# Latent attention by pairs of heads: another order of work on TensorE, VectorE and ScalarE

## What is computed

```python
def mla_queries(h, w_q_a, q_a_norm, w_q_b, q_nope_norm, q_rope_norm, cos, sin):
    c_q = rms_norm(h @ w_q_a, q_a_norm)
    q = (c_q @ w_q_b).reshape(bsz, seq, N_HEADS, QK_DIM)
    q_nope = rms_norm(q[..., :QK_NOPE_DIM], q_nope_norm)
    q_rope = apply_rope(rms_norm(q[..., QK_NOPE_DIM:], q_rope_norm), ...)
...
    def one_block(args):
        s = jnp.einsum('bhqd,bhkd->bhqk', q_blk, k).astype(jnp.float32) * scale
        s = jnp.where(key_pos[None, :] <= query_pos[:, None], s, NEG_INF)
        p = jax.nn.softmax(s, axis=-1).astype(v.dtype)
        return jnp.einsum('bhqk,bhkd->bhqd', p, v)
...
            o = causal_block_attention(q, k_shared, v_shared)
            x = x + o @ mla_w_o[j]
```

## Time and profile before

| | |
|---|---|
| median of 3 runs | 1831.97 us (1831.77 to 1832.18) |
| the profiled execution | 1831.05 us, of which 1829.2 us are its span |
| TensorE busy | 1752.6 us, 96% of the span |
| VectorE, ScalarE busy | 68%, 51% |
| the stretch from the first unit to the third column of the output product | 599.98 to 811.14 us |

### The profile page before, as it was taken

The page is one execution under the profiler, slowest core; times in us unless marked ns, Lnnn a source line. Parts: engine busy times, 40 slices in busy tenths (PEclk is TensorE's granted clock), DMA queues, the critical chain, the costliest instruction groups (busy, mean ns, idle before and its releaser), DMA issues.

```text
span 1829.2 us, 27614 instructions
## 1 busy us (share of the span) xinstructions
PE 1752.6 (96%) x10382; PEld 1430.3 (78%) x10382; DVE 1239.3 (68%) x1895; ACT 926.6 (51%) x1692; POOL 486.0 (27%) x383
## 2 busy tenths in 40 slices
PE   9999999999999877799999999999999999999997
PEld 6778799999887655568999988868766777866675
DVE  8964588886436756657888854476675677567657
ACT  6624466654225655546656532233466733356763
POOL 0960266763000000004767610033000202200010
PEclk9999999999999988999999999999999999999998
DMA  6323223233332110002232333323111123211111
GB/s 215 103 73 92 92 82 116 93 116 108 96 102 89 58 35 24 12 33 83 93 116 94 114 107 95 101 84 109 59 58 58 47 81 101 96 58 58 47 58 58
DMA packets 56464, 151.74 MB, mean 83 GB/s; under 512 B 16768, under 2 KB 18720, under 8 KB 56336
## 3 DMA queue, kind: packets, MB, share of 16 engines
q1 hardware_dynamic: 52816, 147.45, 24.6%
q0 software_dynamic: 3520, 2.57, 0.6%
HBM read 142.84 MB, written 4.19 MB: 80 GB/s over the span
## 4 chain that ended last, share of the span: by engine, by line
PE 82%; DVE 9%; ACT 4%; POOL 3%; issue 2%; DMA 0%; SPq 0%; DVEq 0%; ACTq 0%; POOLq 0%
PE bank L2495 10%; PE bank L2497 10%; PE bank L2496 10%; PE bank L2708 7%; PE bank L2710 7%; PE bank L2709 7%; PE bank L3080 3%; PE bank L3082 3%; PE bank L3081 3%; PE bank L3033 2%; PE bank L3062 2%; PE bank L3063 2%; PE bank L3064 2%; PE bank L2788 1%; DVE wl L1572 1%
## 5 line engine op out<-in xcount | busy, mean ns | idle before, releaser
L1572 DVE TENSOR_TENSOR wl<-raw,wh 128x1024 fp32r<-128x1024 f32 (+2 forms) x183 | 230.2, 1258 | 262.5 <-ACT wh L862 258.4
L862 ACT ACTIVATE wh<-raw 128x1024 fp32r<-128x1024 f32 (+2 forms) x183 | 188.6, 1030 | 354.6 <-PE bank L2497 288.2
L2495 PE MATMUL bank<-hidH,wh 128*128 128x512 f32 x352 | 137.4, 390 | 0.0
L2496 PE MATMUL bank<-hidL,wh 128*128 128x512 f32 x352 | 137.0, 389 | 0.0
L2497 PE MATMUL bank<-hidH,wl 128*128 128x512 f32 x352 | 136.9, 389 | 0.0
L2708 PE MATMUL bank<-xH,wh 128*128 128x256 f32 x480 | 135.8, 283 | 0.0
L2709 PE MATMUL bank<-xL,wh 128*128 128x256 f32 x480 | 135.8, 283 | 0.0
L2710 PE MATMUL bank<-xH,wl 128*128 128x256 f32 x480 | 135.8, 283 | 0.0
L773 POOL TENSOR_TENSOR raw<-raw,wsum 128x512 f32<-128x512 f32 x40 | 86.5, 2164 | 115.2 <-DVE wl L1901 115.2
L3080 PE MATMUL bank<-xH,wh 128*128 128x512 f32 x256 | 111.2, 435 | 6.0 <-ACT qk L1435 3.1
L3082 PE MATMUL bank<-xH,wl 128*128 128x512 f32 x256 | 100.8, 394 | 0.0
(11 more groups left out here) (525 smaller groups left out, 5133.1 us busy)
## 6 DMA issues: line engine op xcount, KB each, us to landing
raw<-w_gu_dram SPq DMA_DIRECT2D x88, 512.0 KB, 3.8
raw<-w_p_dram SPq DMA_DIRECT2D x64, 512.0 KB, 3.3
raw<-w_dn_dram SPq DMA_DIRECT2D x32, 448.0 KB, 3.4
raw<-w_glu_dram SPq DMA_DIRECT2D x16, 512.0 KB, 3.5
raw<-w_dn_dram SPq DMA_DIRECT2D x16, 512.0 KB, 3.6
raw<-w_out_dram SPq DMA_DIRECT2D x16, 512.0 KB, 3.2
raw<-w_in_dram SPq DMA_DIRECT2D x8, 512.0 KB, 7.6
raw<-w_o_dram SPq DMA_DIRECT2D x8, 512.0 KB, 3.2
```

What stands on the lines that cost most here:

```text
L862: nc.scalar.activation(wh[:, (st.base + u) % 2, 0:kts * P], raw[:, (st.base + u) % 4, 0:kts * P], ACT.Copy).then_inc(w_high, 1)
L1572: nc.vector.tensor_tensor(wl[:, s, 0:kts * P], raw[:, (st.base + u) % 4, 0:kts * P], wh[:, s, 0:kts * P].bitcast(F32), ALU.subtract).then_ ...
L2495: nc.tensor.matmul(bank, wh[:, s, w], hi[:, k, :], start=first and kt == 0, stop=False)
L2496: nc.tensor.matmul(bank, wh[:, s, w], lo[:, k, :], start=False, stop=False)
```

## The change

All three engines' programs for this stage are written in another order; nothing is added to what is computed.

- The loop goes by **pairs**, and once more behind the last pair (steps out of range return at once). On TensorE, scores of block j now stand ahead of the transposes of the other head's block, the transposes of blocks 2 and 3 stand in a row, `weigh` of the pair before stands in the first half of the pair (its left half right behind the first scores), `turn_keys` in the middle of the pair instead of its end.
- The 18 units are at five places of a pair (`UNIT_IN`: 5, 5, 4, 2, 2 in pairs 0 to 4). Their sums and roots have four small buffers instead of two.
- Splits of weight blocks are at six places (`SPLIT_IN`).
- 12 slices of the output product are at four places of pairs 5, 6 and 7 (`OUTPUT_IN`); the last four follow the last `weigh`, now by turns of both columns.
- In the stretch before the loop, units, values, queries and keys alternate otherwise; ScalarE's squares run up to two units ahead of the roots, and the rope rows are written later.

```diff
+UNIT_IN = {}
+_at = 3 * QT + 2
+for _p, _slots in enumerate(((0, 1, 2, 3, 4), (0, 1, 2, 3, 4), (0, 1, 3, 4), (1, 3), (1, 3))):
...
+OUTPUT_IN = {(5, 0): (0, 0), (5, 1): (0, 1), (5, 2): (0, 2), (5, 3): (0, 3), (6, 0): (1, 0), (6, 1): (1, 1), (6, 2): (1, 2), (6, 3): (1, 3),
...
-    unit_sum = mla.tensor("unit_sum", [P, 2, 8])
+    unit_sum = mla.tensor("unit_sum", [P, 4, 8])
...
-            for h in range(NH):
...
+            for pair in range(NH // 2 + 1):
+                first, second = 2 * pair, 2 * pair + 1
+                units = [UNIT_IN.get((pair, slot)) for slot in range(5)]
+                scores(second, 0)
+                weigh(pair - 1, left)
+                unit(units[0])
+                scores(second, 1)
+                turn_probs(first, 0)
+                turn_queries(first + 2)
+                scores(second, 2)
+                output_in(pair, 0)
+                unit(units[1])
+                turn_probs(first, 1)
+                scores(second, 3)
+                turn_probs(first, 2)
+                turn_probs(first, 3)
+                weigh(pair - 1, right)
+                output_in(pair, 3)
+                turn_keys(pair + 2)
+                scores(second + 1, 0)
+                unit(units[2])
+                turn_probs(second, 0)
+                scores(second + 1, 1)
+                turn_probs(second, 1)
+                output_in(pair, 1)
+                unit(units[3])
+                turn_queries(second + 2)
+                scores(second + 1, 2)
+                turn_probs(second, 2)
+                turn_probs(second, 3)
+                scores(second + 1, 3)
+                output_in(pair, 2)
+                unit(units[4])
+            for k in range(6, KD):
+                for u in range(2):
+                    output_part(u, range(k, k + 1))
```

VectorE's and ScalarE's new loops follow the same pairs. VectorE's, without the units:

```diff
+                take_sums(first, three)
+                share_probs(first, 0)
+                row_least(second, 0)
+                share_probs(first, 1)
+                take_sums(first, last)
+                share_probs(first, 2)
+                share_probs(first, 3)
+                row_least(second, 1)
+                take_queries(first + 2)
+                row_least(second, 2)
+                split_in(pair, 0)
+                row_least(second, 3)
+                take_sums(second, three)
+                copy_turned(first)
+                share_probs(second, 0)
...
```

More of the change, by code:

```diff
@@ L1273, in copy_turned, with split_in @@
                   .then_inc(sem("turned_act"), 1)
[L1275 to L1285, removed]
+            def split_in(pair, slot):
+                if (pair, slot) in SPLIT_IN:
+                    ahead(st, 0, SPLIT_IN[pair, slot] - 2, True)
+            unit_square(0)
+            unit_square(1)
+            root_of_unit(0)
+            root_of_unit(1)
+            unit_square(2)
+            unit_square(3)
+            ahead(st, 0, 0, True)
+            root_of_unit(2)
+            unit_square(4)
+            root_of_unit(3)
+            unit_square(5)
+            root_of_unit(4)
+            latent_root(2)
+            unit_square(6)
+            root_of_unit(5)
+            unit_square(7)
+            root_of_unit(6)
+            ahead(st, 0, 1, True)
+            unit_square(8)
+            unit_square(9)
+            for n in (7, 8, 9):
+                root_of_unit(n)
+            unit_square(10)
             store_values(0)
             store_values(1)
-            take_keys(0)
+            root_of_unit(10)
+            unit_square(11)
+            ahead(st, 0, 2, True)
             store_values(2)
+            root_of_unit(11)
             store_values(3)
@@ L2121, in _ @@
-            scale_unit(3 * QT - 1)
+            unit_sums(1)
+            scale_unit(0)
+            ahead(stages["a"], 0, 5, True)
+            unit_sums(2)
+            scale_unit(1)
+            unit_sums(3)
+            ahead(st, 0, 0, True)
+            unit_sums(4)
+            scale_unit(2)
+            unit_sums(5)
+            scale_unit(3)
+            scale_unit(4)
+            unit_sums(6)
+            scale_unit(5)
+            unit_sums(7)
+            scale_unit(6)
+            ahead(st, 0, 1, True)
@@ L2974, in _ @@
-            weigh(NH // 2 - 1, range(QT))
-            output_part(0, range(6, KD))
-            output_part(1, range(4, KD))
+            turn_queries(1)
+            values(3)
+            pe.wait_ge(sem("lat_ready"), 7)
+            nc.tensor.matmul(banks[6][:, :], mean_of("fold"), T[:, 3, :], start=True, stop=True).then_inc(sem("krope_folded"), 1)
+            values(4)
+            turn_keys(0)
+            values(5)
+            unit(12)
+            scores(0, 0)
+            unit(13)
+            scores(0, 1)
@@ new lines, in _ @@
+            scores(0, 2)
+            values(6)
+            turn_keys(1)
+            scores(0, 3)
+            values(7)
+            left, right = range(0, 2), range(2, QT)
+            for pair in range(NH // 2 + 1):
+                first, second = 2 * pair, 2 * pair + 1
+                units = [UNIT_IN.get((pair, slot)) for slot in range(5)]
+                scores(second, 0)
[28 more added lines that the diff above has]
+                unit(units[4])
```

283 lines of the change are left out of this document (159 added, 124 removed).

## The result

| | before | with the change |
|---|---|---|
| median of the runs | 1831.87 us (4 runs, 1831.04 to 1832.18) | **1776.30 us** (4 runs, 1776.03 to 1777.13) |
| ratio | | **0.9698**, 95% interval 0.9681 to 0.9715 |
| profiled execution, its span | 1831.05, 1829.2 us | 1777.13, 1775.4 us |

The kernel is 55.6 us faster. The forecast was 1789 us with a range of 1779 to 1803: right in sign and mechanism, wrong in size.

A forecast was written before the change was run, and what follows sets the result against it. No engine full: three orders wait for one another, leaving TensorE idle, then slower. Loop 120.3 + 2.4 + 6 + 1.8 = 130.5 us (37.1 less), stretch before 5.6 less: 42.7 off 1831.05, 1788.4; median 1789 us, range 1779 to 1803.

The forecast's parts named there:

- TensorE's work in the loop: Heads' loop and output product's first two columns: scores, transposes, weighing, queries, keys, units and slices sum to 120.3 us.
- Six keys' waits of 0.4: In the loop, queries wait 0.4 us for ScalarE's keys in each of six pairs: 2.4 us.
- The walk: Stepping pair 5 without units through the new order with measured latencies: 11.7 us; likewise pair 0, 14.5, and pair 1, 18.1.
- 6 us "for what a walk with every engine prompt leaves out": Allowance added to the loop, most of it in pairs 0 to 2: 6 us.
- The turns at the end: Before the output product's column 2, one slice lies over a split of 2.5 us: 1.8 us new wait.
- The stretch before: Stretch before the loop: 33.7 us of work plus 4.3 of waits, 38.0 us, so 5.6 less.
- Pairs without units: Late pairs of the loop take 11.7 us without slices, with 0.4 of wait; 0.75 us for each slice.
- (a): Rival: VectorE and ScalarE set the pace in the pairs with units; 14 us of difference stays, 1799 us; chance 0.16.
- (b): Rival: the keys' wait only moves and stays at 15.1 us, 12.7 more than taken, 1802 us; chance 0.06.
- (c): Rival: slower; scores ahead of other head's transposes make a ring through three queues in 16 heads, 1842 us; chance 0.03.
- (d): Rival: no change, if the stretch behind the loop needed the time for weights or POOL's sums; chance 0.02.
- covered twice: TensorE's 0.75 us wait for shares in every head: covered once by weighing, once by weighing, keys and scores.

The follow-up runs named there:

- experiment 3: Changed kernel with no output slice in the pairs, all sixteen behind the last pair by column: 1776.92 us, ratio 0.9702.
- small dose on VectorE: Changed kernel with VectorE's taking of the queries done twice for fourteen heads: 1778.51 us, ratio 0.9708.
- experiment 5: Changed kernel with both halves of the weighing together again, at the place of the right half: 1781.53 us, ratio 0.9724.
- experiments 4, 5 and 6: Changed kernel with keys at each pair's end (4): 1776.99 us; VectorE's queries taken twice (6): 1778.51 us; or least values twice (6): 1791.57 us.
- experiment 7's first run: Changed kernel with the old loop put back, keeping the new stretch before it and the four small buffers: 1822.76 us, ratio 0.9945.

## Why the size was wrong

By the prediction's own steps, in the profiled executions (forecast 42.7 us less, measured 53.8):

- **TensorE's work in the loop**, forecast 120.3: measured 120.04 - 1.55 = 118.5. Right to 1.8 us. Four slices made pair 5 2.66 us longer than it is without them in experiment 3's trace (14.15 against 12.10 less a wait of 0.61), 0.67 each, so 12 x 0.75 was 1.0 too much. The scores of head 12 take 0.28 + 0.50 + 0.71 + 0.92 = 2.4 us and those of head 11 2.7, where 2.6 was taken for every head.
- **Six keys' waits of 0.4**, forecast 2.4: none. The walk was of a pair without slices and units, and there it holds: experiment 3, without slices, has this wait in pair 5 (0.6 us). But all six pairs with keys have something between keys and queries, pairs 0 to 4 a unit and pair 5 a slice (719.81 above, 0.8 us). One pair's wait was charged six times.
- **6 us "for what a walk with every engine prompt leaves out"**: none. **This is the step that failed**, with 6 of the 11.1 us missed. It rested on VectorE's 49.2 us of work in the first three pairs against TensorE's 48.6. In the new loop VectorE has 13.30 + 16.53 + 14.28 = 44.1 us there in a length of 47.5, 93%, and TensorE is busy for all of it. A full second engine is a reason for suspicion, not a wait; no row and no step of the walk named the wait that the 6 us would be.
- **The turns at the end**, forecast 1.8: 1.55. What the step left out: behind this wait the clock fell in the profiled run, which cost 1.1 us more (below).
- **The stretch before**, forecast 38.0: 35.51, its work 33.9 for 33.7 as worked out, its waits 1.6 instead of 4.3.
- **Pairs without units**, forecast 11.7 us with 0.4 of wait, and 0.75 for each slice: pair 5 has 12.10 with 0.6 of wait in experiment 3's trace, and 14.15 with four slices and no wait in the changed kernel's.

Together: 1.8 + 2.4 + 6.0 + 0.25 in the loop and 2.5 before it are 12.95 us; less 1.6 behind and 0.2 ahead of it, 11.1. The range failed in the same place. Its low end took off the 6 us and 1.3 of the start but kept 2.4 + 3.0, though the room that the text itself worked out, 47.3 + 9.9 us, allowed 1774.7. Where a walk shows hardly a wait, the bound by work is a likely end, not an unlikely one. Of the signs that the text gave for being right, the clock, the waits for keys and shares and the wait before column 2 came out as said; the loop did not, at 120 us for 126 to 134.

Of the rivals, (a) is refuted by the list of waits and the small dose on VectorE, (b) and (c) by the list of waits, (d) by the result. Two readings of the rows were wrong, without weight for the sum. The wait of 0.75 us for shares stands in six of the sixteen heads and not in every one. And the pair from 759.68 on, at clock 1.00, had no short waits ahead of it: it begins right behind one of 3.30 us. That the shares' wait would be "covered twice" held; experiment 5 shows that the order's left half of the weighing covers something else as well, which the walk contained but the text did not name.

## What to carry to other kernels

Where three in-order engines hand a few banks round, price a new order by the bounding engine's work alone, walk one period with measured latencies, and add only waits that the walk shows, for the periods that it stands for; an allowance without a row is a guess. Moving one step of such a ring moves the wait to the engine whose turn was hidden behind it, so here tests of one move understated the whole. Once the loop is at the bound, look where a block's split is covered by too little: there 1.4 and 0.9 us were to be had.

## What the runs showed of the hardware

The same wait before column 2 (1.55 us, the same instruction, the same work ahead of it) was followed by the low clock in one trace and not in another. The changed kernel, then the one with the queries taken twice:

```profile
755.71 0.47 PE L2572 MATMUL bank<-kvH,wh 128*128 128x512 f32 x1 [1.55 <-DVE wl L1616]
...
757.68 0.63 PE L2574 MATMUL bank<-kvH,wl 128*128 128x512 f32 x1
758.10 0.63 PE L2572 MATMUL bank<-kvH,wh 128*128 128x512 f32 x1
```

```profile
758.06 0.47 PE L2574 MATMUL bank<-kvH,wh 128*128 128x512 f32 x1 [1.55 <-DVE wl L1616]
...
759.99 0.39 PE L2576 MATMUL bank<-kvH,wl 128*128 128x512 f32 x1
760.22 0.39 PE L2574 MATMUL bank<-kvH,wh 128*128 128x512 f32 x1
```

Matmuls at 0.63 us and 0.42 apart against 0.39 and 0.23 apart: 1.2 GHz until 759.4 in the first, 2.4 GHz in the second. Of the five traces with this wait (experiments 4, 5 and 6 are the others) two had it and three had not. Behind it the rest of the program took 1019.7 us in those two and 1018.6 to 1018.8 in the three, so it costs about 1.1 us in the end. The 1777.13 us of the changed kernel's profiled run, against three others at 1776.0 to 1776.6, fits this but does not show it. The old loop has longer cases. In the trace of the kernel before, the lower clock stands behind a wait of 3.02 us (739.71) and not behind one of 3.30 (759.68); in the trace of experiment 7's first run the wait of 3.30 at the same step has it. The Trainium skill (TensorE: Matmul & The Clock Gate, section "What's actually happening") has the clock follow how busy the engine has recently been. The traces agree that it falls only behind or during waits of TensorE; from 600 us until just behind the start of column 2, no run's trace has a fall without one. That the length of the single wait decides it they do not bear out.
